# The mixer's output projection of a transformer layer: from 64 products over the whole depth to seven half-size products for each pair of token tiles

## The chip, the cores and the metric

One core of a Trainium2 chip runs the whole kernel. The metric is device time in microseconds of one execution, as the median of several. TensorE (PE) multiplies, VectorE (DVE), ScalarE (ACT) and GpSimd (POOL) compute elementwise, and SyncE (SP), ACT and POOL issue DMA transfers.

## The reference, cut to what matters

One layer: 512 prompt tokens and 8 sample tokens of width 1024, float32.

```
pool_out  = causal pooling of u, a linear map per group        # 512 columns
mlstm_out = sigmoid(og) * norm(mlstm heads) * mlstm_norm_g     # 512 columns
mix = concat([pool_out, mlstm_out]) @ w_out                    # the changed part
x = layer_norm(ALPHA * x + mix, ln1_g, ln1_b)
qc = x @ ca_wq      # cross attention follows, then a mixture of experts
```

## The kernel before

Tokens lie in five tiles: prompt tiles 0, 1, 2 and 4 of 128 rows, and tile 3 (`SAMPLES`) of 8. `mixT` holds the mixed values transposed, eight blocks of 128 channels: blocks 0 to 3 are the pooled half, written by ACT (L1516), blocks 4 to 7 the heads, written by VectorE (`take_heads`, L1979). Weights come in column blocks of 1024 x 512 (2 MB) into a ring `wring` of three slots: SP issues them in order (`block_load`, L1206), each when the block three earlier has been used. `w_out` is the blocks wo0 and wo1; the slot of block `u` is next filled with wq0.

The projection of a tile is two banks (one for each 512 columns of the output), each eight products of 128x128 by 128x512. A float32 product stands in the trace as two records. Tile 0 is written out by hand (`wo_steps`, L787): its first halves run before and after the last pooling product (`pool_product(3, 1)`, L746) and the turning of the states (`turn_states`, L757, record L761). Tiles 1, 2 and 4 use `rows_project` (L765, record L773). Between them stand the transposes of finished tiles (`transpose_x`, L541, record L548), two small ones for the samples (L812, L819), and the samples' own projection (`rows_samples`, L777, record L782). Then comes the query projection, itself seven half-size products for two halves of the tokens (`product`, L587, record L611); its product 6 needs sums of tokens (`sum_tokens`, L1790) and of weights (`sum_weights`, L1771) that VectorE makes.

VectorE takes each bank with `residual` (L2054): ALPHA times x plus the bank (L2062) and statistics of 512 columns (L1740), twice a tile, and then `norm` (L1742): aggregate (L1750), center and scale by gain (L1752), wait for GpSimd's inverse deviation (`norm_rstd`, L2550), scale and add (L1761). Between the tiles stand the samples' head output (L2082 to L2096), the samples' mixed values (L2101) and three sums of wq0. `bank_d` hands three PSUM banks (ps3 to ps5) round: PE waits until VectorE has freed the bank of three uses ago. MBANK, ps6 and ps7, is idle here.

GpSimd's program is in order: for each sample it loads a state (`load_state`, L2596: 256 KB and 512 KB), waits for VectorE's `carried` (L1984) and updates the state (`update_state`, L2603: three operations and a store). Between these stand `window_sums` (L2615), which VectorE's `pool_diff(0)` needs, and `head_rstd(3)` (L2587), which the last heads need. After sample 6 it loads the gain and bias vectors of the first norm (L2670, L2671), stores the states and loads state 7.

The order around the change comes from these in-order programs and their semaphores alone. Tile 0's start on PE is, cut:

```python
wo_steps(wo_banks[0], "wo0", (4, 5, 6, 7))
pool_product(3, 1)
turn_states()
wo_steps(wo_banks[1], "wo1", (4, 5, 6, 7))
pe.wait_ge(act_free, at["pool"])
```

## Time and profile before

| | us |
|---|---|
| three runs, median (lowest to highest) | 663.36 (663.21 to 664.26) |
| the profiled execution | 662.14 |
| its span, first to last instruction | 660.4 |
| PE busy, DVE busy, POOL busy in it | 630.5, 345.6, 204.6 |

The profiled execution's own time is 1.7 us above its span, and 1.2 us below the median. Times in rows count from the start of the span. A chain of waits follows the last instruction back to whatever released each step.

### The profile page before, as it was taken

The page shows a single profiled execution, that of the slowest core. Times are in us where ns is not written, and L with a number is a line of the kernel's source. Part 1 is how long each engine was busy: PE and PEld are TensorE (multiplying, and loading weights), DVE is VectorE, ACT ScalarE, POOL GpSimd, SP SyncE. Part 2 cuts the span into 40 slices and gives each one's busy share as a digit, 9 for nine tenths or more (in the row PEclk, how much of TensorE's full clock was granted, in tenths as well). Part 3 has the DMA queues.
Part 4 walks back from the last instruction along what each step waited for, and adds up shares of the span by engine and source line. Part 5 has one row for each costly group of instructions (what it writes and reads, how often), then busy time and mean ns, then how long its engine had stood idle before and what let it go on. Part 6 is the DMA issues. An engine that isn't in the chain of part 4 may idle for free.

```text
span 660.4 us, 8621 instructions
## 1 busy us (share of the span) xinstructions
PE 630.5 (95%) x3216; PEld 387.4 (59%) x3216; DVE 345.6 (52%) x803; ACT 152.5 (23%) x334; POOL 204.6 (31%) x240
## 2 busy tenths in 40 slices
PE   6999999999999999999999999989999999999992
PEld 3445588887888864446888774444564444333331
DVE  0283356326556960857643865355873334244465
ACT  1113221001544120002002640222324111121144
POOL 5241010100577735412002984102244432111221
PEclk9999999999999999999999999999999999999997
DMA  8994478613335357104705977544449999999797
GB/s 301 393 327 168 144 168 223 233 54 127 101 88 200 113 191 129 47 0 149 297 0 189 346 276 276 223 164 188 200 152 359 414 411 416 383 362 415 270 192 157
DMA packets 45667, 146.07 MB, mean 221 GB/s; under 512 B 5594, under 2 KB 5786, under 8 KB 41519
## 3 DMA queue, kind: packets, MB, share of 16 engines
q1 hardware_dynamic: 31847, 108.29, 44.0%
q0 software_dynamic: 11600, 32.24, 18.4%
q10 hardware_dynamic: 2176, 4.96, 2.0%
q8 instruction: 27, 0.44, 0.3%
q14 instruction: 17, 0.14, 0.1%
HBM read 130.27 MB, written 20.33 MB: 228 GB/s over the span
## 4 chain that ended last, share of the span: by engine, by line
PE 78%; DMA 9%; DVE 6%; issue 2%; POOL 2%; ACT 1%; ACTq 0%; DVEq 0%; POOLq 0%
PE ps L611 15%; PE ps L773 14%; PE ps L520 9%; PE ps L1115 7%; PE ps L484 6%; PE ps L1135 4%; PE ps L609 4%; DMA P<-x_d,smp 3%; PE ps L792 2%; DMA xn<-y_d 2%; PE ps L876 2%; PE ps L860 1%; PE ps L667 1%; PE ps L548 1%; DMA P<-in_cache_mem_v 1%
## 5 line engine op out<-in xcount | busy, mean ns | idle before, releaser
L773 PE MATMUL ps<-wring,P 128*128 128x512 f32 x224 | 99.4, 596 | 0.0
L773 PEld LDWEIGHTS ps<-wring,P 128*128 128x128 f32 x224 | 41.5, 190 | 49.4 <-issue 49.3
L1115 PE MATMUL ps<-wring,P 128*32 128x512 f32 (+1 forms) x288 | 63.6, 593 | 0.9 <-DVE P L2386 0.9
L1810 DVE SCALAR_TENSOR_TENSOR P<-ps,P 128x264 f32<-128x264 f32 (+1 forms) x70 | 28.8, 427 | 60.9 <-PE ps L611 44.3
L520 PE MATMUL ps<-wring,P 128*128 128x512 f32 x128 | 58.1, 612 | 1.0 <-DVE P L1765 0.8
L484 PE MATMUL ps<-xT,wring 128*128 128x312 f32 (+1 forms) x256 | 57.5, 383 | 0.0
L2556 POOL TENSOR_SCALAR rstd<-agg 128x1 f32<-128x1 f32 (+1 forms) x15 | 15.7, 1049 | 117.9 <-DVE agg L1750 117.9
L484 PEld LDWEIGHTS ps<-xT,wring 128*128 128x128 f32 x256 | 46.4, 190 | 9.3
L2386 DVE COPY P<-ps 128x512 f32<-128x512 f32 x11 | 7.6, 692 | 74.3 <-PE ps L1096 66.8
L520 PEld LDWEIGHTS ps<-wring,P 128*128 128x128 f32 x128 | 24.7, 196 | 31.2 <-issue 31.0
L1115 PEld LDWEIGHTS ps<-wring,P 128*32 128x32 f32 (+1 forms) x288 | 21.6, 128 | 35.0 <-issue 34.9
L2699 POOL TENSOR_TENSOR P<-P,xT 128x2048 f32<-128x2048 f32 x8 | 36.1, 4523 | 8.9 <-DMA xT<-sq_d 5.6
L2062 DVE SCALAR_TENSOR_TENSOR xn<-xn,ps 128x512 f32<-128x512 f32 x16 | 10.9, 682 | 45.0 <-PE ps L773 25.4
L1135 PE MATMUL ps<-P 128*32 128x512 f32 (+1 forms) x144 | 32.6, 594 | 0.6 <-issue 0.6
L1400 ACT ACTIVATE xT<-ps 128x512 f32<-128x512 f32 (+1 forms) x30 | 13.9, 518 | 71.6 <-PE ps L548 71.5
L611 PE MATMUL ps<-xT,wring 128*128 128x264 f32 (+1 forms) x128 | 29.6, 387 | 0.0
L611 PE MATMUL ps<-P 128*128 128x264 f32 x128 | 29.5, 385 | 0.0
L611 PE MATMUL ps<-P,wring 128*128 128x256 f32 (+1 forms) x128 | 29.2, 382 | 0.0
L1115 PE MATMUL ps<-xT,P 128*32 128x512 f32 (+1 forms) x96 | 28.2, 593 | 0.0
L611 PEld LDWEIGHTS ps<-P 128*128 128x128 f32 x128 | 24.3, 190 | 4.2
L611 PEld LDWEIGHTS ps<-xT,wring 128*128 128x128 f32 x128 | 23.8, 190 | 4.8 <-issue 1.1
L611 PEld LDWEIGHTS ps<-P,wring 128*128 128x128 f32 x128 | 24.2, 190 | 3.8
(447 smaller groups left out, 1092.3 us busy)
## 6 DMA issues: line engine op xcount, KB each, us to landing
wring<-in_w_in SPq DMA_DIRECT2D x5, 2048.0 KB, 9.7
wring<-in_w_gate SPq DMA_DIRECT2D x10, 1024.0 KB
wring<-in_w_up SPq DMA_DIRECT2D x10, 1024.0 KB
P<-in_w_down SPq DMA_DIRECT2D x10, 1024.0 KB, 12.0
P<-in_cache_mem_k SPq DMA_DIRECT2D x8, 1024.0 KB, 6.6
P<-in_cache_mem_v SPq DMA_DIRECT2D x8, 1024.0 KB, 5.1
y_d<-P POOLq DMA_DIRECT2D x1, 4160.0 KB, 31.9
wring<-in_ca_wv SPq DMA_DIRECT2D x2, 2048.0 KB, 20.9
```

Source lines behind the costliest of these rows:

```text
L484: last = mm(out, lhs(k), rhs(k), start=(k == 0), stop=(k == n - 1))
L520: last = mm(bk[:, :], memT[:, k, m * 128:m * 128 + 128], w[:, k, :], start=(k == 0), stop=(k == KC - 1))
L609: last = mm(bank[:, 0:n], x[:, k, 128 * i:128 * i + 128], w[:, k, :], start=(k == 0), stop=(k == 3))
L611: last = mm(bank[:, 0:n], w[:, k, 128 * i:128 * i + 128], x[:, k, :], start=(k == 0), stop=(k == 3))
L773: last = mm(bk[:, :], src[:, k, START[t]:START[t] + TR], w[:, k, :], start=(k == 0), stop=(k == KC - 1))
L792: last = mm(bank[:, :], mixT[:, k, 0:TR], w[:, k, :], start=(k == 4), stop=(k == 1))
L1115: last = mm(GU[p % 2][lo:lo + m, :].rearrange("p (g f) -> p g f", g=2), xgT[:, p % 3, k, lo:lo + m], gu[s][:, :, k, :], start=(k == 0), st ...
L1135: last = mm(YB[q][lo:lo + m, :], hT[:, p % 2, f, lo:lo + m], dn[s][:, f, q * 512:q * 512 + 512], start=(f == 0), stop=(f == 1))
L1400: A(xT[:, 4 * q:4 * q + 4, START[t]:START[t] + n], bk[:, 0:4 * n].rearrange("p (k c) -> p k c", k=4), ACT.Copy).then_inc(act_free, 1)
L1810: V.scalar_tensor_tensor(dst, src, scale, part, ALU.mult, ALU.add).then_inc(part_added, 1)
L2556: link(G.tensor_scalar(x, agg[0:n, 1:2], LN_EPS, None, ALU.add))
L2699: G.tensor_tensor(x, x, qb[:, b % 4:b % 4 + 1].broadcast_to([128, 2, D]), ALU.mult).then_inc(kq_done, 1)
```

## The change

The four prompt tiles become two pairs, (0, 1) and (2, 4). For a pair, the two tiles and the two halves of the depth make a 2x2 block matrix, and so do the halves of depth and of columns of `w_out`. Seven block products (four 128x128 by 128x512 products each) take the place of eight: `first`, `second` and `fourth` use the mixed values as they are, `fifth`, `sixth`, `third` and `seventh` use sums of them, which VectorE makes (`sum_mixed`, four operations a pair). The weight sums are made by DMA: SP loads a quarter of `w_out` (1 MB) into each of four places, when the keys, values and the block u there have been used, and GpSimd issues transfers that add further quarters to them: two to `wo_sums[6]`, one each to 7 and 5, and the finished sum 6 to 4. `first` and `fifth` go to MBANK and ACT copies them out. VectorE puts the seven results together with eleven operations of 512 columns for a pair, in place of four. PE starts with both `second` and both `first` products, then waits for sums 5 and 7. The load of wq0 now waits for both `fifth`. The norm vectors are issued by ACT after the states, and state 7 is loaded before the last adding transfer. `TOKENS`, the semaphores' names and the counts of `gb_in` follow suit.

```diff
+        block_at = lambda lo: view(lo, 2048, "p (k c) -> p k c", k=4)
+        wo_sums = {6: block_at(2144), 7: block_at(4224), 4: block_at(8384), 5: wring[:, 2, 0:4, :]}
+        mixed = lambda t, hf: mixT[:, 4 * hf:4 * hf + 4, START[t]:START[t] + TR]
+        spare = [view(512 * i, 512) for i in range(4)], [sgT[:, i, 0:512] for i in range(4)]
...
+        first_part, fifth_part = [view(lo, 512) for lo in (10448, 10960)], [view(lo, 512) for lo in (13540, 14052)]
+        sum_part, all_part = view(11472, 512), view(12484, 512)
+        PAIRS = ((0, 1), (2, 4))
...
+        chain_made, sums_made = sem("chain_made"), sem("sums_made")
+        T2_HALF, T2_MADE, T4_MADE, T3_P_MADE = 16, 32, 48, 32
...
-            def wo_steps(bank, name, ks):
-                w = wring[:, BI[name] % WR]
-                for k in ks:
-                    if k == 7:
-                        pe.wait_ge(dve_free, at["heads", 3])
-                    last = mm(bank[:, :], mixT[:, k, 0:TR], w[:, k, :], start=(k == 4), stop=(k == 1))
-                return last
-
-            pe.wait_ge(dve_free, at["heads", 2])
-            for name in WO:
-                use_block(name)
-            wo_banks = [bank_d() for name in WO]
-            wo_steps(wo_banks[0], "wo0", (4, 5, 6, 7))
+            wo0, wo1 = [wring[:, BI[name] % WR] for name in WO]
+            def mixed_product(bank, x, w, done):
+                for k in range(4):
+                    last = mm(bank[:, :], x[:, k, :], w[:, k, :], start=(k == 0), stop=(k == 3))
+                last.then_inc(done, 1)
+            def first(i):
+                mixed_product(MBANK[i], mixed(PAIRS[i][0], 0), wo0[:, 0:4], act_full)
...
+            def second(i):
+                mixed_product(bank_d(), mixed(PAIRS[i][0], 1), wo0[:, 4:8], dve_full)
...
+            def fifth(i):
+                pe.wait_ge(xsum_done, MIXED[i] + 1)
+                pe.wait_ge(act_free, at["first", i])
+                mixed_product(MBANK[i], mixed_sums[i][5], wo_sums[5], act_full)
...
+            def sixth(i):
+                pe.wait_ge(xsum_done, MIXED[i] + 2)
+                mixed_product(bank_d(), mixed_sums[i][6], wo_sums[6], dve_full)
+            def third(i):
+                pe.wait_ge(xsum_done, MIXED[i] + 3)
+                mixed_product(bank_d(), mixed_sums[i][3], wo1[:, 4:8], dve_full)
+            def seventh(i):
+                pe.wait_ge(xsum_done, MIXED[i] + 4)
+                mixed_product(bank_d(), mixed_sums[i][7], wo_sums[7], dve_full)
+            def fourth(i):
+                mixed_product(bank_d(), mixed(PAIRS[i][1], 1), wo_sums[4], dve_full)
+            pe.wait_ge(dve_free, at["heads", 3])
+            use_block("wo0")
+            second(0)
+            second(1)
             pool_product(3, 1)
             at["pool"] = na[0]
             turn_states()
-            wo_steps(wo_banks[1], "wo1", (4, 5, 6, 7))
             pe.wait_ge(act_free, at["pool"])
-            for name, bank in zip(WO, wo_banks):
-                wo_steps(bank, name, (2, 3, 0, 1)).then_inc(dve_full, 1)
-            rows_project(1, WO, mixT)
-            transpose_x(0, x1_ready)
+            first(0)
+            first(1)
+            pe.wait_ge(sums_made, T3_P_MADE)
+            fifth(0)
+            fifth(1)
+            used[BI["u"]] = (act_full, na[0])
+            pe.wait_ge(chain_made, T2_MADE)
+            use_block("wo1")
+            sixth(0)
             pe.wait_ge(cq_done, NS)
             bk = bank_d()
             for h in range(H):
                 last = nc.tensor.transpose(bk[0:NS, h * 128:h * 128 + 128], cq[:, h, :], ident)
             last.then_inc(dve_full, 1)
-            rows_project(2, WO, mixT)
+            third(0)
+            seventh(0)
+            pe.wait_ge(chain_made, T4_MADE)
+            fourth(0)
+            sixth(1)
+            transpose_x(0, x1_ready)
+            third(1)
+            seventh(1)
             transpose_x(1, x1_ready)
             pe.wait_ge(samples_dve, HEADS_READY)
             bk = bank_d()
@@ -819,7 +870,7 @@
                 last = nc.tensor.transpose(bk[:, h * NS:h * NS + NS], vsn[:, h * 128:h * 128 + 128], ident[0:NS, 0:NS])
             last.then_inc(dve_full, 1)
             samples_mixed = nd[0]
-            rows_project(4, WO, mixT)
+            fourth(1)
             transpose_x(2, x1_ready)
             pe.wait_ge(dve_free, samples_mixed)
             rows_samples(WO, mixT)
...
-            for i in range(3, BI["wc0"] + 1):
+            for i in range(3, BI["wq0"]):
+                block_load(i)
+            low, high = [[w[:, 0:4], w[:, 4:8]] for w in (BLOCKS[BI["wo0"]][1], BLOCKS[BI["wo1"]][1])]
+            sp.wait_ge(dve_full, at["keys", 3])
+            sp.dma_start(wo_sums[6], high[1]).then_inc(piece_in[0], 16)
+            sp.dma_start(wo_sums[7], high[0]).then_inc(piece_in[1], 16)
+            sp.wait_ge(dve_full, at["state", 3])
+            sp.dma_start(wo_sums[4], low[1]).then_inc(piece_in[2], 16)
+            sp.wait_ge(act_full, at["u", 1])
+            sp.dma_start(wo_sums[5], low[0]).then_inc(piece_in[2], 16)
+            for i in range(BI["wq0"], BI["wc0"] + 1):
                 block_load(i)
...
             take_states()
+            act.dma_start(gb[:, 0, :], a["ln1_g"][0].partition_broadcast(128)).then_inc(emb_in, 16)
+            act.dma_start(gb[:, 1, :], a["ln1_b"][0].partition_broadcast(128)).then_inc(emb_in, 16)
...
+            def copy_part(dst, bank):
+                nf[0] += 1
+                act.wait_ge(act_full, nf[0])
+                A(dst, bank[:, :], ACT.Copy).then_inc(act_free, 1)
+
+            for part in (first_part, fifth_part):
+                for i in range(2):
+                    copy_part(part[i], MBANK[i])
...
-            dve.wait_ge(gb_in, 32)
-            residual(0, x1_ready)
...
+            def sum_mixed(i):
+                (t, u), s, done = PAIRS[i], mixed_sums[i], MIXED[i]
+                V.tensor_tensor(s[5], mixed(u, 0), mixed(u, 1), ALU.subtract).then_inc(xsum_done, 1)
+                dve.wait_ge(xsum_done, done + 1)
+                V.tensor_tensor(s[6], s[5], mixed(t, 0), ALU.subtract).then_inc(xsum_done, 1)
+                dve.wait_ge(xsum_done, done + 2)
+                V.tensor_tensor(s[3], s[6], mixed(t, 1), ALU.add).then_inc(xsum_done, 1)
+                V.tensor_tensor(s[7], mixed(t, 0), mixed(u, 0), ALU.subtract).then_inc(xsum_done, 1)
+            def take_second(i):
+                x, bk = quarter_of(PAIRS[i][0], 0), full()
+                V.scalar_tensor_tensor(x, x, ALPHA, bk[:, :], ALU.mult, ALU.add).then_inc(dve_free, 1)
+                dve.wait_ge(dve_free, nf[0])
+
+            def take_first(i):
+                x = quarter_of(PAIRS[i][0], 0)
+                dve.wait_ge(act_free, at["first", i])
+                link(V.tensor_tensor(x, x, first_part[i], ALU.add))
+
+            def take_fifth(i):
+                dve.wait_ge(act_free, at["fifth", i])
+                for t in PAIRS[i]:
+                    x = quarter_of(t, 1)
...
+                link(last)
+
+            def take_sixth(i):
+                bk, x = full(), quarter_of(PAIRS[i][0], 1)
+                V.tensor_tensor(sum_part, bk[:, :], first_part[i], ALU.add).then_inc(dve_free, 1)
+                dve.wait_ge(dve_free, nf[0])
+                link(V.tensor_tensor(x, x, sum_part, ALU.subtract))
+            def take_third(i):
+                bk, x = full(), quarter_of(PAIRS[i][0], 1)
+                V.tensor_tensor(x, x, bk[:, :], ALU.add).then_inc(dve_free, 1)
...
+            def take_seventh(i):
+                bk, u = full(), PAIRS[i][1]
+                V.tensor_tensor(all_part, bk[:, :], sum_part, ALU.add).then_inc(dve_free, 1)
+                x = quarter_of(u, 0)
+                V.scalar_tensor_tensor(x, x, ALPHA, all_part, ALU.mult, ALU.add)
+                x = quarter_of(u, 1)
+                link(V.tensor_tensor(x, x, all_part, ALU.subtract))
+                statistics(u, 1)
+            def take_fourth(i):
+                bk, x = full(), quarter_of(PAIRS[i][1], 0)
+                V.tensor_tensor(x, x, bk[:, :], ALU.add).then_inc(dve_free, 1)
...
+            take_second(0)
+            take_second(1)
+            dve.wait_ge(act_free, at["pool"])
+            sum_mixed(0)
+            sum_mixed(1)
+            take_first(0)
+            statistics(0, 0)
+            take_first(1)
+            take_fifth(0)
+            take_fifth(1)
             carried(7)
-            residual(1, x1_ready)
+            take_sixth(0)
...
+            take_third(0)
+            dve.wait_ge(emb_in, 64)
+            norm(0, x1_ready, first_known=True)
...
-            residual(2, x1_ready)
+            take_seventh(0)
+            take_fourth(0)
+            norm(1, x1_ready, first_known=True, last=0)
+            statistics(2, 0)
+            take_sixth(1)
+            take_third(1)
+            norm(2, x1_ready, first_known=True)
+            take_seventh(1)
...
-            residual(4, x1_ready, between=[lambda n=n: sum_weights("wq0", n) for n in (1, 2, 3)])
+            for n in (1, 2, 3):
+                sum_weights("wq0", n)
+            take_fourth(1)
+            norm(4, x1_ready, first_known=True, last=0)
             residual_samples("mixed rows", x1_ready)
...
             update_state(4)
+            pool.wait_ge(piece_in[0], 32)
+            pool.dma_start(wo_sums[6], low[0], accum_op=ALU.add).then_inc(chain_made, 16)
+            pool.wait_ge(piece_in[1], 32)
+            pool.dma_start(wo_sums[7], high[1], accum_op=ALU.add).then_inc(sums_made, 16)
             window_sums()
             update_state(5)
             head_rstd(3, TR, NQT)
+            pool.wait_ge(chain_made, T2_HALF)
+            pool.dma_start(wo_sums[6], high[0], accum_op=ALU.add).then_inc(chain_made, 16)
             load_state(6)
+            pool.wait_ge(piece_in[2], 48)
+            pool.dma_start(wo_sums[5], high[0], accum_op=ALU.add).then_inc(sums_made, 16)
             update_state(6)
+            load_state(7)
+            pool.wait_ge(chain_made, T2_MADE)
+            pool.dma_start(wo_sums[4], wo_sums[6], accum_op=ALU.add).then_inc(chain_made, 16)
...
-            pool.wait_ge(act_full, at["states"])
-            norm_vectors("ln1_g", "ln1_b")
             states_out()
-            load_state(7)
...
-            norm_rstd(0)
             update_state(7)
-            norm_rstd(1)
             head_rstd(4, NS, H)
-            for t in (2, 4, SAMPLES):
+            for t in (0, 1, 2, 4, SAMPLES):
```

## Rows read from the trace of the kernel before

**Rows 1.** The page: busy time of the engines, and the clock in 40 slices
```profile
PE 630.5 (95%) x3216; PEld 387.4 (59%) x3216; DVE 345.6 (52%) x803; ACT 152.5 (23%) x334; POOL 204.6 (31%) x240
PEclk9999999999999999999999999999999999999997
```
**Rows 2.** Chain of waits, 195 to 340 us: start, length, what
```profile
246.72 10.30 PE ps L792 x24
257.03 13.94 PE ps L773 x32
```
**Rows 3.** Order of time on TensorE, 190 to 330 us: start, length, what, idle before
```profile
238.51 0.66 PE L699 MATMUL ps<-con,P 128*128 128x128 f32 x4 [1.11 <-DVE P L1976]
...
245.25 1.04 PE L750 MATMUL ps<-P,poolw 128*128 128x312 f32 x4
...
321.45 7.31 PE L611 MATMUL ps<-P 128*128 128x264 f32 x32
```
**Rows 4.** VectorE's groups, 262 to 322 us: count | busy us, mean ns | idle before
```profile
L1740 DVE BATCH_NORM_STATS2 st<-xn 128x6 f32<-128x512 f32 x8 | 5.6, 695 | 0.3
L1752 DVE SCALAR_TENSOR_TENSOR xn<-xn,agg,gb 128x1024 f32<-128x1024 f32 x4 | 5.5, 1369 | 0.1
L2062 DVE SCALAR_TENSOR_TENSOR xn<-xn,ps 128x512 f32<-128x512 f32 x8 | 5.4, 680 | 22.5 <-DMA gb<-in_ln_b 16.4 <-PE ps L773 6.1
L1761 DVE SCALAR_TENSOR_TENSOR xn<-xn,rstd,gb 128x1024 f32<-128x1024 f32 x4 | 5.1, 1284 | 3.7 <-POOL rstd L2557 3.7
```
**Rows 5.** Order of time on VectorE, 205 to 330 us
```profile
229.73 1.47 DVE L2009 SCALAR_TENSOR_TENSOR P<-P 128x496 f32<-128x496 f32 x1
...
236.38 0.68 DVE L2009 SCALAR_TENSOR_TENSOR P<-P 128x496 f32<-128x496 f32 x1
...
245.72 0.29 DVE L1988 CUSTOM_DVE_ANT_0 P<-P 128x128 f32<-128x128 f32 x1 [1.69 <-DMA P<-qk_d]
...
277.20 0.67 DVE L2082 TENSOR_TENSOR P<-ps,sg 8x512 f32<-8x512 f32 x1
...
280.22 0.37 DVE L2090 BATCH_NORM_AGGREGATE hagg<-hst 8x2 f32<-8x6 f32 x4
282.05 1.10 DVE L2096 TENSOR_SCALAR smp<-smp,hagg,den 8x128 f32<-8x128 f32 x4 [1.47 <-POOL den L2588]
...
291.07 0.62 DVE L2101 SCALAR_TENSOR_TENSOR P<-ps,colv,P 128x8 f32<-128x8 f32 x4
...
307.24 1.21 DVE L2072 SCALAR_TENSOR_TENSOR xn<-xn,P 8x1024 f32<-8x1024 f32 x1 [0.93 <-ACT P L1524]
...
314.07 1.22 DVE L1796 TENSOR_TENSOR P<-xT 128x1024 f32<-128x1024 f32 x1
...
320.08 0.19 DVE L1799 TENSOR_TENSOR P<-xT,P 128x32 f32<-128x32 f32 x1
```
**Rows 6.** Order of time on GpSimd, 195 to 330 us
```profile
227.19 1.03 POOL L2617 TENSOR_TENSOR P<-P 128x512 f32<-128x512 f32 x1
...
232.62 0.78 POOL L2613 DMA_DIRECT2D out<-P  x1 [0.29 <-POOL P L2611]
235.94 0.22 POOL L2587 TENSOR_SCALAR den<-hagg 128x4 f32<-128x4 f32 x1 [2.54 <-DVE hagg L1968]
...
237.26 0.82 POOL L2600 DMA_DIRECT2D P<-in_state_mlstm_C  x1
```
**Rows 7.** DMA issues: queue, count, KB each, median us from issue to landing
```profile
wring<-in_ca_wq SPq DMA_DIRECT2D x2, 2048.0 KB, 9.0
xn<-y_d POOLq DMA_DIRECT2D x6, 512.0 KB, 8.2
```
**Rows 8.** Stretches: length, busy us of PE, PEld, DVE, ACT, POOL, clock, DMA share, GB/s
```profile
242.00:244.00 2.00, 2.00 (x6) 0.80 (x6) 1.86 (x7) 0.51 (x2) 0.00 (x0) 1.00 1.00 365
244.00:246.00 2.00, 2.00 (x8) 1.14 (x7) 0.31 (x4) 0.03 (x1) 0.00 (x0) 1.00 0.99 386
...
630.00:642.00 12.00, 12.00 (x65) 4.70 (x66) 7.67 (x15) 4.70 (x9) 3.21 (x4) 1.00 1.06 202
```

More of the change, by code:

```diff
@@ L313, in layer_kernel @@
         mem_in = [sem(f"mem_in{m}") for m in range(2)]
-        wk_in = [sem(f"wk_in{q}") for q in range(3)]
+        piece_in = [sem(f"piece_in{q}") for q in range(3)]
         HALF_MEMORY, CONSTANTS = 16, 32
         ident_ready, con_in, x_in, gb_in, small_in, cache_in = [sem(s) for s in ("ident_ready", "con_in", "x_in", "gb_in", "small_in", "cache_in")]
+        chain_made, sums_made = sem("chain_made"), sem("sums_made")
+        T2_HALF, T2_MADE, T4_MADE, T3_P_MADE = 16, 32, 48, 32
         wgr_in, st_in, emb_in = sem("wgr_in"), sem("st_in"), sem("emb_in")
@@ L410, in layer_kernel @@
         SUMMED = {name: 4 * i for i, name in enumerate(("q", "k", "v", "wq0", "wq1"))}
-        TOKENS = {name: 4 if name[0] == "w" else 0 for name in SUMMED}
+        MIXED = (4, 8)
+        TOKENS = {name: 12 if name[0] == "w" else 0 for name in SUMMED}
         part_banks = [ps[6], ps[7], ps[3], ps[4], ps[5]]
@@ L516, in memory_block @@
                         if k < 6:
-                            pe.wait_ge(wk_in[k // 2], 16)
+                            pe.wait_ge(piece_in[k // 2], 16)
                         else:
@@ L1740, in statistics, with norm @@
                 return V.bn_stats(st_of(t)[:, 6 * q:6 * q + 6], xn[0:rows_of(t), t, q * 512:q * 512 + 512])
-            def norm(t, signal, finish=True, first_known=False, meanwhile=None):
+            def norm(t, signal, finish=True, first_known=False, meanwhile=None, last=1):
                 n = rows_of(t)
@@ L1747, in norm @@
                     statistics(t, 0)
-                link(statistics(t, 1))
+                link(statistics(t, last))
                 pows[0] += 1
@@ new lines, in take_second @@
+            def take_second(i):
[10 more added lines that the diff above has]
+                    x = quarter_of(t, 1)
+                    last = V.scalar_tensor_tensor(x, x, ALPHA, fifth_part[i], ALU.mult, ALU.add)
+                link(last)
@@ L2250, in list_rows @@
                 V.tensor_copy(dst[0:rows, :, n], r[:, 89:91]).then_inc(dst_ready, 1)
-            dve.wait_ge(gb_in, 64)
+            dve.wait_ge(gb_in, 32)
             def choose_now(n):
@@ L2661, in _ @@
                 masks(h + 2)
+            low, high = [[w[:, 0:4], w[:, 4:8]] for w in (BLOCKS[BI["wo0"]][1], BLOCKS[BI["wo1"]][1])]
             update_state(4)
+            pool.wait_ge(piece_in[0], 32)
+            pool.dma_start(wo_sums[6], low[0], accum_op=ALU.add).then_inc(chain_made, 16)
+            pool.wait_ge(piece_in[1], 32)
+            pool.dma_start(wo_sums[7], high[1], accum_op=ALU.add).then_inc(sums_made, 16)
             window_sums()
```

15 lines of the change are left out of this document (12 added, 3 removed).

## The prediction

> **What bounds the kernel now.** I read the page first: TensorE is busy 95% of the span, at the full granted clock in all slices but the last [rows 1]. The chain of waits confirms it around the change: it runs on TensorE from 246.72 to 270.97 us with nothing between the products, 32 records (16 products) in 13.94 us [rows 2]. The order of time on TensorE then gives the dates: the last wait before the stretch is 1.11 us at 238.51, for VectorE's last heads; the fourth pooling product stands at 245.25; and product 6 of the query projection, the first that needs sums from VectorE, starts at 321.45 without a wait [rows 3]. VectorE's order of time shows how near it is to that date: its last token sum starts at 320.08 and takes 0.19 [rows 5]. So VectorE has 1.2 us in hand there and no more, although it is idle for 22.5 us before its reading of the banks [rows 4]: idle early, on a stalled norm vector, and nearly full late. Its late load is what decides this change, along with the transfers.
>
> I make the sum for the start of product 6, because everything after it hangs on TensorE as before and should move with it.
>
> **TensorE.** A product costs 13.94/16 = 0.87 or 10.30/12 = 0.86 us [rows 2]; four cost 3.45. Eight fewer save 6.9. Now second(0) starts at 241.8 (3.45 before the pooling product of 245.25 [rows 3]), both seconds end at 248.7, the pooling product takes 1.04 and the turning of the states 0.43 (from 246.29 to 246.72, where products go on [rows 2, 3]). The old order had four products between the states and the wait for ACT's copy of the pooled half. Now only the states cover it; the copy I put at 0.6, an estimate below VectorE's 0.68 for 512 columns [rows 4], so 0.2 us of wait appear and first(0) starts at 250.3. Both firsts end at 257.2, fifths at 264.1, sixth(0) at 267.6 if nothing is late. By TensorE alone product 6 would start at 321.45 - 6.9 + 0.2 = 314.75.
>
> **VectorE.** From the end of sixth(0) its program is dense. Its work up to the last token sum:
> - fourteen operations of 512 columns at 0.70 with their waits for themselves (0.680 each [rows 4]): 9.8. Before, the whole projection had eight such operations; now it has twenty-two, eight of them earlier
> - seven statistics of 0.695 [rows 4]: 4.9
> - four norms: aggregate 0.21 with its gap, 1.30, a wait of 3.7/4 = 0.9 for GpSimd, 1.28 [rows 4]: 14.7
> - the samples' head output, 277.20 to 280.59, 3.4, and its scaling 1.0 (four records in 1.10): 4.4; mixed values of samples 0.62 [rows 5]
> - three sums of wq0 at 1.22 (the same shape as the 1.22 of 314.07 [rows 5]): 3.7
> - the sample rows and two parts of the query product, 307.24 to 314.07 [rows 5]: 6.8
> - the sums from 314.07 to 320.27 [rows 5]: 6.2
>
> That is 51.1. From 267.6 it ends at 318.7, and at 318.9 with the stops at the banks that I get by laying both programs side by side. TensorE would be there at 314.75. So VectorE becomes the bound: 4.1 of the 6.7 us are lost to it, as waits of TensorE for the samples' mixed values before the samples' projection, for the bank of fourth(1) and the norm of tile 4, and before product 6. With transfers in time the gain is 321.45 - 318.9 = 2.5.
>
> The early operations (two seconds, eight sums, two firsts, one statistics, four of the fifths) are hidden in the idle time of 16.4 us [rows 4]. They start late, though, behind carried(6); see below.
>
> **The transfers.** No transfer adds in this stretch before. The nearest rows are the adding ones at the end (512 KB each): between 630 and 642 us the 16 engines are full (share 1.06) and move 202 GB/s, where plain loads move 365 and 386 [rows 8]. 1 MB (1.049) then costs 5.2 us to add and 2.75 to load. Bounds: 2.75 below, as if adding were free; above, the 8.2 us to landing of half a MB [rows 7], so 16. I take 5.2, the rate of full engines, since these will be full too.
>
> GpSimd's order now: update 4 ends at 227.1 (the next record stands at 227.19 [rows 6]), then the first part of sum 6 and sum 7 are issued, some 0.8 to 1.0 each as its other issues [rows 6]. window_sums and update 5 come 2.0 later, update 5's store is issued by 235.4 instead of 233.4 and head_rstd(3), which waits for VectorE until 235.94 [rows 6], is still not delayed: this part costs nothing by 0.5 us. Then the second half of sum 6, state 6, sum 5 and only then update 6. On the engines, from 229.1 (2 us after the issue): four adding MBs before the fifths may start (6, 7, 6, 5) 20.8; two loads (4 and 5) 5.5; update 5's store 0.7; state 6, 0.79 MB, 2.1. That is 29.1, so 258.2. ACT issues the norm vectors (1 MB) at about 251 on its own queue; if they share, half of them, 1.4, come ahead; landing takes 0.7: sum 5 is there at 260.3. The fifths were due at 257.2. **TensorE waits 3.1 us there**, and since VectorE's dense part starts behind sixth(0), all of it counts.
>
> That queues share is what state 6 shows before: issued at 237.26 [rows 6], beside wq0's 2 MB at 9.0 us to landing [rows 7], it released VectorE only at 245.72 [rows 5], when both together, 2.9 MB at 375 GB/s, had had their 7.7 us. The Trainium skill ("DMA: Bandwidth & Descriptors", Queues, rings and completion order) says that an engine goes round its queues packet by packet. By strict order of issue instead, sum 5 would be 1.4 us earlier and the time 662.6.
>
> State 6 itself now lands near 253.7, carried(6) ends at 254.6, the seconds are read by 256.0 and the first sum is made by 256.7, in time for 260.3. Eight sums end at 261.6, the fifths are read by 269.5 and carried(7) is done by 270.4, just before sixth(0) ends at 270.7. State 7 waits for update 6's store, which stands behind sum 5 (about 261), is issued by 263 and takes 2 + 2.1: landing at 267, for a need at 269.5. The load of wq0 starts at 267 instead of 237 and is needed near 300; 9.0 us to landing hide it. Sum 4 (from SBUF, bounded as above) is issued near 264 and due at 278. The norm vectors are due at 276. SP's waits hold back only its own pieces and wq0.
>
> Beside update 6, VectorE's operations can be slower: L2009 took 1.47 with GpSimd at work and 0.68 without [rows 5]. For the eight sums I put up to 3 us on this, and it eats the slack before carried(7) but not more; for update 7 beside the samples' work I add 0.3. The Trainium skill ("SBUF — State Buffer", Who interferes with whom) says that a VectorE instruction with two SBUF inputs contends with a GpSimd one that reads SBUF; the trace agrees (1.47 against 0.68), and by the rule without slack the time would be 2 to 3 us higher.
>
> **Sum.** The count of 51.1 gives 318.7 + 3.1 + 0.3 = 322.1 against 321.45, +0.65; with the stops at the banks it is 322.3, +0.85. I take the count: 662.14 + 0.65 = 662.8 for the profiled execution. It stood 1.2 below the median of the runs, so 664.0.
>
> **Rivals.**
> - *The transfers are in time.* Adding at 4.4 us for a MB or less brings sum 5 to 257. VectorE's dense part alone bounds: -2.5, 660.8. For it: the share of 1.06 [rows 8] counts packets of other transfers too, and the 202 GB/s may hold waits. Against: 202 GB/s was steady over 12 us.
> - *The adding transfers are slower (the other side).* Their rows are of 2 KB, half of what the measured ones carry. At 5.8 us for a MB sum 5 lands 2.4 later, at 262.7, and TensorE waits 5.5 before fifth(0): 666.4. It decides from 261.0 on: 0.7 us beyond my date are enough to be measurably slower. For it: head, store and state transfers stand in the same queue, and every delay of one is handed to the next; against: with smaller pieces the plain loads are as fast.
> - *TensorE alone bounds*, since the sums or the transposes leave VectorE more room than I count: 321.45 to 314.75, 656.7. Against it stands the 1.2 us of slack [rows 3, 5] which fourteen operations where eight stood (and the norm of tile 0 behind them) must use up.
>
> **Numbers.** About 0.2% (1.3 us) is what a measurement of this kernel can tell from no change, so 662.0 to 664.7. The forecast (wait of 2 to 4.2 us, 662.9 to 665.1) 0.38, of which 0.32 lies within 0.2% and 0.06 above; slower transfers 0.33; transfers in time 0.22; TensorE alone 0.07. That gives faster 0.29, same 0.32, slower 0.39. The range of 8 in 10 takes in the transfers in time down to 660.4 and the slower ones up to 667.6 (a wait of 6.7), and leaves out TensorE alone and the rest of the slower ones.
>
> **What would show it.** In the profile after: the idle time before fifth(0) on TensorE, released by the adding transfer into the slot of u, 3 us (0 and over 5 are the rivals); carried(6) near 254; VectorE without idle time but for GpSimd's inverse deviations from sixth(0) on; waits of TensorE for VectorE before the samples' projection, the query's first product and product 6. If product 6 starts before 317 or no wait is seen in front of it, the count of VectorE's work is wrong; if heads 3 starts later than 238.5, so is the claim that GpSimd's two issues are free.

## The result and the profile after

The changed kernel took 673.29 us (median of 5 runs, 671.81 to 681.25) where the kernel before took 663.36 (660.39 to 667.97): a ratio of 1.0166, 95% interval 1.0126 to 1.0207. That is slower than the forecast, than its range and than the price of the rival on the slow side. A run over 1.5% above the fastest of its kernel is left out of the ratios and of the medians given here; of the changed kernels only experiment 2 has one (678.55 us). The profiled execution was the longest of the five. At 330 us it is 1.1 us behind the profile of the unchanged repeat below, which took 673.3; the rest of its excess lies behind 430 us, outside the change (a wait of 2.48 us for a sample's value cache that the repeat has not, and a granted clock of 0.91 from 500 to 540 us, where the repeat has 1.00).

The page of the changed kernel, the lines that answer to [rows 1]:

```profile
PE 636.0 (94%) x3200; PEld 389.5 (57%) x3200; DVE 364.2 (54%) x825; ACT 155.1 (23%) x338; POOL 210.5 (31%) x243
PEclk9999999999999988998999999989989999999996
```

TensorE has 16 records fewer (8 products of two records), and yet is busy 5.5 us longer. A good part of that belongs to this long execution: in the repeat it is busy 629.8 us, 0.7 less than before, where eight products fewer are worth 6.9. The clock line says why one must not read "busy" as "work": apart from the last slice, which was low before too, five slices are below 0.90. Those of 238 to 272 and 306 to 323 us lie at the change, the two behind 430 us outside it. The order of time on TensorE shows which records paid (start, length, what, idle before):

```profile
241.51 1.12 PE L710 MATMUL ps<-con,P 128*128 128x128 f32 x4 [3.38 <-DVE P L2048]
242.42 3.07 PE L761 MATMUL ps<-P,poolw 128*128 128x312 f32 x8
...
254.80 7.13 PE L803 MATMUL ps<-wring,P 128*128 128x512 f32 x16
266.34 9.95 PE L803 MATMUL ps<-wring,P 128*128 128x512 f32 x16 [4.41 <-DMA wring<-in_w_out]
...
309.64 5.27 PE L793 MATMUL ps<-wring,P 128*8 128x256 f32 x64 [2.09 <-DVE P L2246]
...
330.76 7.41 PE L622 MATMUL ps<-P 128*128 128x264 f32 x32
```

Product 6 of the query projection starts at 330.76, against 321.45 in [rows 3]: 9.3 us, nearly the whole 9.9 of the times (0.7 of it stood already at 205 us, ahead of the change). In the repeat it is 8.2 of 9.2. Three waits are seen: 3.38 for VectorE's heads (1.11 before), 4.41 for weight sum 5, 2.09 for the samples' mixed values. Behind the second the same 16 records that took 7.13 at 254.80 take 9.95. The stretches of the changed kernel (length, busy us of PE, PEld, DVE, ACT, POOL, clock, DMA share, GB/s):

```profile
240.00:244.00 4.00, 2.49 (x8) 2.12 (x9) 2.17 (x7) 0.23 (x1) 1.41 (x2) 0.66 1.08 288
252.00:256.00 4.00, 3.85 (x15) 2.19 (x14) 0.00 (x0) 1.39 (x3) 1.30 (x1) 1.00 0.61 215
256.00:260.00 4.00, 4.00 (x10) 1.71 (x9) 3.72 (x12) 0.60 (x1) 2.72 (x3) 1.00 1.01 254
260.00:264.00 4.00, 1.94 (x5) 0.57 (x3) 3.93 (x5) 0.60 (x1) 1.74 (x2) 1.00 1.10 200
264.00:268.00 4.00, 1.66 (x2) 0.84 (x3) 3.30 (x6) 0.00 (x0) 0.72 (x1) 0.65 0.48 123
268.00:272.00 4.00, 4.00 (x6) 1.69 (x5) 0.00 (x0) 0.00 (x0) 4.00 (x8) 0.50 0.87 251
```

Behind both long waits TensorE runs for a while at its lower level, 0.50 of full speed, 1.2 of 2.4 GHz: the mean of 240 to 244 is 0.66, and behind the wait for sum 5 it is 0.50 through all of 268 to 272. At that level there are 6 records in the 4 us, where 272 to 276 at full clock has 10.

The chain of waits tells which of the three waits led to the end:

```profile
231.11 7.03 PE ps L495 x32
238.16 16.14 DMA wring<-in_w_out
254.30 0.37 issue
254.67 11.63 DMA wring<-in_w_out
266.34 13.39 PE ps L803 x24
279.76 0.70 DVE P L2178
```

It does not pass through the heads at all. It leaves TensorE at 238.16, when the block u is done and SP may load quarter 5 into its place, goes with that load for 16.14 us, with the adding transfer into it for 11.63, through fifths and sixth(0), and then onto VectorE, as forecast. GpSimd's order of time shows what it did meanwhile:

```profile
229.13 1.29 POOL L2815 DMA_DIRECT2D P<-in_w_out  x1 [0.48 <-DMA P<-in_w_out]
229.91 1.58 POOL L2765 TENSOR_TENSOR P<-P 128x512 f32<-128x512 f32 x1
230.91 1.57 POOL L2757 TENSOR_TENSOR P<-P,wcb 128x512 f32<-128x512 f32 x1
231.91 1.56 POOL L2758 TENSOR_TENSOR P<-P,vsT 128x512 f32<-128x512 f32 x1
...
246.33 0.79 POOL L2748 DMA_DIRECT2D P<-in_state_mlstm_C  x1 [4.92 <-DMA out<-P]
...
254.67 1.30 POOL L2823 DMA_DIRECT2D wring<-in_w_out  x1 [6.98 <-DMA wring<-in_w_out]
```

It waits 4.92 us for the store of update 5, which stands behind adding transfers, 6.98 for load 5 and, at 267.28, 5.24 for the store of update 6. Beside the three operations from 229.91 to 233.47, one operation of VectorE, which took 1.47 in [rows 5], takes 4.67:

```profile
229.35 4.67 DVE L2081 SCALAR_TENSOR_TENSOR P<-P 128x496 f32<-128x496 f32 x1
```

The transfers issued between 220 and 285 us (queue, count, KB each, median us to landing):

```profile
P<-in_w_out SPq DMA_DIRECT2D x3, 1024.0 KB, 8.1
P<-in_w_out POOLq DMA_DIRECT2D x3, 1024.0 KB, 14.0
...
wring<-in_w_out SPq DMA_DIRECT2D x1, 1024.0 KB, 16.1
...
wring<-in_w_out POOLq DMA_DIRECT2D x1, 1024.0 KB, 11.6
```

A plain load of 1 MB takes 16.1 us here, where wq0's 2 MB took 9.0 in [rows 7]. Sum 5's own transfer is the last row, issued at 254.67. What the queues moved from 256 to 260 us (packets, MB, share) shows that it hardly ran in that time; q10 carries the norm vectors that ACT issued at 254.70 and 255.08, q0 is GpSimd's:

```profile
q10 hardware_dynamic: 265, 0.99, 96.1%
q0 software_dynamic: 15, 0.03, 4.9%
```

### The profile page after: what moved, and what is told of

The parts are those of the page before. It is cut to its first block, busy times and chain, and to the rows that moved or that the text cites. A ratio compares the mean times of both kernels' runs of the same rounds, so it can differ in the third digit from the quotient of the medians.

```text
span 679.5 us, 8634 instructions
## 1 busy us (share of the span) xinstructions
PE 636.0 (94%) x3200; PEld 389.5 (57%) x3200; DVE 364.2 (54%) x825; ACT 155.1 (23%) x338; POOL 210.5 (31%) x243
## 4 chain that ended last, share of the span: by engine, by line
PE 78%; DMA 9%; DVE 7%; issue 2%; ACT 1%; POOL 1%; DVEq 0%; ACTq 0%; POOLq 0%
PE ps L622 15%; PE ps L1166 11%; PE ps L531 9%; PE ps L495 8%; PE ps L784 7%; PE ps L1186 5%; DMA wring<-in_w_out 4%; PE ps L620 4%; DMA xn<-y_d 2%; PE ps L803 2%; PE ps L927 2%; DMA P<-in_cache_mem_v 2%; PE ps L911 1%; PE ps L1147 1%; PE ps L693 1%
## 5 line engine op out<-in xcount | busy, mean ns | idle before, releaser
L1166 PE MATMUL ps<-wring,P 128*32 128x512 f32 (+1 forms) x288 | 65.4, 600 | 0.9 <-DVE P L2534 0.9
L531 PE MATMUL ps<-wring,P 128*128 128x512 f32 x128 | 58.7, 617 | 1.0 <-DVE P L1837 0.8
L784 PE MATMUL ps<-wring,P 128*128 128x512 f32 x128 | 58.7, 609 | 0.0
L531 PEld LDWEIGHTS ps<-wring,P 128*128 128x128 f32 x128 | 24.9, 198 | 31.6 <-issue 31.3
L784 PEld LDWEIGHTS ps<-wring,P 128*128 128x128 f32 x128 | 24.0, 194 | 28.3 <-issue 28.2
L803 PE MATMUL ps<-wring,P 128*128 128x512 f32 x64 | 31.3, 644 | 4.6 <-DMA wring<-in_w_out 4.4
L2870 POOL DMA_INDIRECT P<-x_d,smp x11 | 11.3, 1031 | 47.4 <-PE ps L1147 28.1
```

What stands on the lines that cost most here:

```text
L531: last = mm(bk[:, :], memT[:, k, m * 128:m * 128 + 128], w[:, k, :], start=(k == 0), stop=(k == KC - 1))
L784: last = mm(bk[:, :], src[:, k, START[t]:START[t] + TR], w[:, k, :], start=(k == 0), stop=(k == KC - 1))
L803: last = mm(bank[:, :], x[:, k, :], w[:, k, :], start=(k == 0), stop=(k == 3))
L1166: last = mm(GU[p % 2][lo:lo + m, :].rearrange("p (g f) -> p g f", g=2), xgT[:, p % 3, k, lo:lo + m], gu[s][:, :, k, :], start=(k == 0), st ...
```

## The experiments

Each was run beside the kernel before on the same chip, so ratios are against that. "Heads" is the start of the first record of L710 (TensorE's turning of the last heads). Where a kernel leaves something out, its expectation says so.

**1. The changed kernel once more**, no edit.

> The changed kernel once more, to have a typical profile of it. Both theories: 672 us, with the same three waits of TensorE (about 3.4 us before the last heads, 4.4 before fifth(0), 2 before the samples' projection). If each of these waits is followed by a stretch at half the clock again, the lowered clock belongs to the waits; if the heads come back to 238.5 us, the 3 us lost there were chance.

Measured: 673.20 us, ratio 1.0119 (1.0050 to 1.0187). The heads start at 240.56, not at 238.5. The heads' wait is 3.13 us, that for sum 5 is 4.67 with 9.71 us for the 16 records behind it, and product 6 starts at 329.62. The picture repeats. One thing differs: behind the same wait of 2.09 us the samples' projection takes 3.64 us at full clock, not 5.27, and yet product 6 is as late behind it (21.13 us from start to start, 21.12 in the first profile), because TensorE then waits for VectorE instead. This third loss of clock costs nothing.

**2. No wait for the weight sums**, all transfers still made.

```diff
-                mixed_product(MBANK[i], mixed_sums[i][5], wo_sums[5], act_full)
+                mixed_product(MBANK[i], mixed_sums[i][5], wo0[:, 0:4], act_full)
...
-            pe.wait_ge(sums_made, T3_P_MADE)
...
-            pe.wait_ge(chain_made, T2_MADE)
...
-            pe.wait_ge(chain_made, T4_MADE)
```

The sixths, sevenths and fourths take plain quarters in the same way. So that no quarter is overwritten too early, the edit also adds waits for the sums elsewhere: SP waits for sums 5 and 7 ahead of wq0 and for sum 4 ahead of wq1, and VectorE for sum 4 ahead of its sums of wq0, which it starts at 302.02 without a wait.

> All loads and adding transfers run as in the change, but TensorE multiplies by plain quarters of w_out and waits for no sum, so the projection's values are not the reference's. My theory (the wait for the adding transfers, 4.4 us, and the half clock behind it, 3 us more, are the larger part of the loss): no wait before fifth(0), no lowered clock there, 7 us less than the changed kernel, 665. Rival (the traffic and GpSimd's issues slow the kernel by themselves, and the wait only stands where VectorE would have been late anyway): 670 or more.

Measured: 667.31 us, ratio 1.0048 (1.0010 to 1.0085). TensorE:

```profile
240.21 1.12 PE L710 MATMUL ps<-con,P 128*128 128x128 f32 x4 [3.12 <-DVE P L2048]
241.12 3.67 PE L761 MATMUL ps<-P,poolw 128*128 128x312 f32 x8
...
254.81 17.43 PE L803 MATMUL ps<-wring,P 128*128 128x512 f32 x40
...
323.29 2.06 PE L622 MATMUL ps<-P 128*128 128x264 f32 x8 [0.17 <-DVE P L1871]
```

The wait before the fifths and its lowered clock are gone, and product 6 moves from 329.6 to 323.3: 6.3 us. The heads stay late, with another VectorE operation held, one of 16 columns this time:

```profile
228.69 4.15 DVE L2082 TENSOR_TENSOR P<-P 128x16 f32<-128x16 f32 x1
```

**3. No weight sums at all**: as 2, and the four loads and five adding transfers are left out.

```diff
-            pool.dma_start(wo_sums[6], low[0], accum_op=ALU.add).then_inc(chain_made, 16)
...
-            pool.dma_start(wo_sums[7], high[1], accum_op=ALU.add).then_inc(sums_made, 16)
```

> As plain_quarters, and the four loads and five adding transfers are left out too, so the values are not the reference's. My theory: the heads are back at 238.5 us after a wait of 1.1, state 6 lands by 246, and only VectorE's dense program of 51 us behind sixth(0) bounds: 661 (2.5 us below the kernel before). Rival (VectorE's added operations alone make the change lose): 664 or more, with the heads at 238.5.

Measured: 661.31 us, ratio 0.9962 (0.9934 to 0.9990).

```profile
238.94 0.66 PE L710 MATMUL ps<-con,P 128*128 128x128 f32 x4 [1.30 <-DVE P L2038]
...
298.08 5.33 PE L793 MATMUL ps<-wring,P 128*8 128x256 f32 x64 [2.09 <-DVE P L2236]
...
320.05 7.31 PE L622 MATMUL ps<-P 128*128 128x264 f32 x32
```

This is the case that the prediction called "the transfers are in time", priced at 660.8. So the products and VectorE's part were priced well, and all of the loss hangs on how the sums are made: 673.2 to 667.3 by the waits for them, 667.3 to 661.3 by their traffic and issues. The date of product 6 is less of a proof: VectorE's last token sum ends at 319.14, and product 6 starts 0.9 later, since TensorE lost 1.7 us to the clock on the samples' projection (5.33 for 3.64) and waited 0.66 for a block of wq.

**4. The price of a wait by itself**: the kernel before, with TensorE waiting for the norm vectors ahead of tile 1's products.

```diff
+            pe.wait_ge(gb_in, 32)
```

> The kernel before, in which TensorE waits for the norm vectors before tile 1; they landed at 263.0, when it would start at 256.9, and VectorE has room behind it. If a wait of this size also costs clock: 6 us for the wait and some 3 us for a stretch at half the clock behind it, 672. Rival (the half clock in the changed kernel comes from something else than the wait): 6 us alone, 669.5, at the full clock.

Measured: 671.99 us, ratio 1.0133 (1.0071 to 1.0195).

```profile
262.00 17.01 PE L773 MATMUL ps<-wring,P 128*128 128x512 f32 x32 [4.21 <-DMA gb<-in_ln_b]
```

The same records in the order of time of the kernel before:

```profile
256.86 14.10 PE L773 MATMUL ps<-wring,P 128*128 128x512 f32 x32
```

The wait is 4.21 us, and the 32 records behind it take 2.9 us more, by the clock. A wait of 4.2 us costs 7.1; the times differ by 8.0.

**5. The first two adding issues behind the heads' deviations**: experiment 2 with this move on GpSimd.

```diff
             update_state(4)
-            pool.wait_ge(piece_in[0], 32)
-            pool.dma_start(wo_sums[6], low[0], accum_op=ALU.add).then_inc(chain_made, 16)
-            pool.wait_ge(piece_in[1], 32)
-            pool.dma_start(wo_sums[7], high[1], accum_op=ALU.add).then_inc(sums_made, 16)
             window_sums()
             update_state(5)
             head_rstd(3, TR, NQT)
+            pool.wait_ge(piece_in[0], 32)
+            pool.dma_start(wo_sums[6], low[0], accum_op=ALU.add).then_inc(chain_made, 16)
+            pool.wait_ge(piece_in[1], 32)
+            pool.dma_start(wo_sums[7], high[1], accum_op=ALU.add).then_inc(sums_made, 16)
```

> This is plain_quarters (sums of the changed order, TensorE taking plain quarters and waiting for no sum, all adding transfers made) with GpSimd's first two adding issues moved behind head_rstd(3); nothing else differs. My theory: what delays heads 3 by some 1.5 us and more is that these two issues push update 5 against VectorE's work on heads 3, where one VectorE operation of 16 columns was held for 4.1 us; the traffic itself does not slow VectorE. Then heads 3 start near 238.9 as in no_sums, the pooling products run at full clock, and the time is about 664, some 4 below plain_quarters. Rival (the adding traffic slows VectorE or the chip, wherever it is issued): heads 3 stay near 240.5, the clock falls in the same slices and the time stays near 667.5.

Measured: 673.45 us, ratio 1.0137 (1.0094 to 1.0180). The step that it tested came out as I said: VectorE's operations are not held,

```profile
230.33 0.90 DVE L2080 TENSOR_TENSOR P<-P,con 128x16 f32<-128x16 f32 x1
231.26 1.47 DVE L2081 SCALAR_TENSOR_TENSOR P<-P 128x496 f32<-128x496 f32 x1
```

and the heads (at 240.51, the rival's date, but this execution was 1.5 us behind experiment 2's already) follow their predecessors (the first record of L710 one head earlier) by 12.8 us, where it is 14.0 in experiment 2 and 12.2 in experiment 3; behind their wait of 1.91 us the pooling products keep the full clock (1.98 us). My sum for the time was wrong by 9 us, since I left out what the moved issues stand in front of: 

```profile
250.62 1.28 POOL L2821 DMA_DIRECT2D P<-in_w_out  x1 [9.12 <-DMA P<-in_w_out]
251.36 1.31 POOL L2749 DMA_DIRECT2D P<-in_state_mlstm_C  x1
```

State 6 is issued 5 us later than in the changed kernel and lands in 13.3 us, not 9.0. VectorE waits 19.41 us for it to 265.43, makes the sums of mixed values behind it, and TensorE waits 9.66 for those, with half the clock afterwards. A state for which VectorE waits 1.69 us in the kernel before [rows 5], at no cost there, is the bound here.

**6. Less work for VectorE behind sixth(0)**: experiment 3 without six operations of 512 columns.

```diff
-                link(V.tensor_tensor(x, x, sum_part, ALU.subtract))
...
-                V.scalar_tensor_tensor(x, x, ALPHA, all_part, ALU.mult, ALU.add)
-                x = quarter_of(u, 1)
-                link(V.tensor_tensor(x, x, all_part, ALU.subtract))
```

> This is no_sums without six of VectorE's 512-column operations behind sixth(0): the second operation of the sixths' reading and two of the sevenths', in each pair; 6 x 0.70 = 4.2 us less work for VectorE, TensorE's products and all transfers as in no_sums. My theory (VectorE's dense program from the end of sixth(0) sets when product 6 of the query projection can start): product 6 starts 2.5 to 4.2 us earlier than the 320.05 of no_sums and the time is about 657.5. Rival (VectorE's work is not what bounds there, the waits seen are of another chain): product 6 stays within 1 us of 320.05 and the time near 661.

Measured: 657.53 us, ratio 0.9905 (0.9870 to 0.9941), 3.8 below experiment 3 for 4.2 us of work.

```profile
295.79 3.64 PE L793 MATMUL ps<-wring,P 128*8 128x256 f32 x64
...
315.36 4.85 PE L622 MATMUL ps<-P 128*128 128x264 f32 x21
```

No wait stands before the samples' projection any more, and VectorE's last token sum ends at 315.10, not 319.14: 4.0 us for 4.2 us of work. VectorE bounds up to that projection, which starts 2.3 us earlier. Product 6 comes 4.7 us earlier; the other 2.4 are the lowered clock and the wait for wq of experiment 3, both gone here.

**7. The sums by the engines**: GpSimd makes sums 7, 6 and 4, VectorE sum 5; the results are the changed kernel's.

```diff
+            G.tensor_tensor(wo_sums[7], wo1[:, 0:4], wo1[:, 4:8], ALU.add)
...
+            G.tensor_tensor(wo_sums[6], wo_sums[7], wo0[:, 0:4], ALU.add)
+            G.tensor_tensor(wo_sums[4], wo_sums[6], wo0[:, 4:8], ALU.add)
...
+            V.tensor_tensor(wo_sums[5], wo0[:, 0:4], wo1[:, 0:4], ALU.add)
```

> The changed kernel without the transfers for the sums: GpSimd makes sum 7 behind load_state(6), sums 6 and 4 behind load_state(7), in its idle time, and VectorE makes sum 5 in its own before the firsts. The products, their order and the results are those of the changed kernel. My theory (the transfers are what costs; the products by sums are worth a small gain): no wait before fifth(0), no lowered clock, product 6 near 320 and the time about 661.5, as no_sums. Rival (GpSimd's 2048-column sums hold VectorE, or come too late for the fifths and sixths): waits of 1 us and more before the fifths or sixths, product 6 after 321.5 and 664 or more.

Measured: 674.25 us, ratio 1.0146 (1.0114 to 1.0178): the rival. One operation of GpSimd,

```profile
238.34 4.50 POOL L2818 TENSOR_TENSOR P<-wring 128x2048 f32<-128x2048 f32 x1
```

and VectorE's beside it and beside the two later ones:

```profile
237.01 6.70 DVE L2042 TENSOR_SCALAR P<-P,hagg,den 128x128 f32<-128x128 f32 x4
...
265.96 4.51 DVE L2161 TENSOR_TENSOR xn<-xn,P 128x512 f32<-128x512 f32 x1 [1.02 <-ACT P L1589]
270.50 4.89 DVE L2167 SCALAR_TENSOR_TENSOR xn<-xn,P 128x512 f32<-128x512 f32 x1
```

The same operations take 1.12 and 0.69 us in experiment 3. Here the first ends at 243.71, 0.9 behind the end of GpSimd's (242.84), and the second at 270.47, 0.6 behind that of GpSimd's next sum (265.38 and 4.52 long): VectorE is not slowed but stopped. (Its first group is 5.6 us longer than in experiment 3, 1.1 more than GpSimd's operation lasts; no run shows why.) TensorE waits 6.71 us for the heads and runs at half clock behind it. The Trainium skill ("SBUF — State Buffer", SBUF: two separate sides) calls the ports that VectorE and GpSimd share an exclusive lock, kept for a whole instruction; these ends agree.

**8. The same with VectorE's waits filled**: work is put where it waited for GpSimd's inverse deviations.

```diff
-            norm(0, x1_ready, first_known=True)
+            norm(0, x1_ready, first_known=True, meanwhile=scale_heads)
...
-            norm(1, x1_ready, first_known=True, last=0)
-            statistics(2, 0)
+            norm(1, x1_ready, first_known=True, last=0, meanwhile=lambda: statistics(2, 0))
...
+            norm(2, x1_ready, first_known=True, meanwhile=lambda: read_seventh(1))
```

> engine_sums with work of VectorE put into its waits for GpSimd's inverse deviation: the samples' head scaling into the norm of tile 0, the samples' statistics into that of tile 1, the reading of seventh(1) into that of tile 2. My theory (from sixth(0) to product 6 VectorE bounds, and 0.9 us of each norm is a wait that can hold work): product 6 some 2 to 2.5 us earlier than in engine_sums, about 659.3. Rival (TensorE or the heads of the samples bound there, or the moved work delays what TensorE waits for): as engine_sums, 661.5.

Measured: 670.78 us, ratio 1.0093 (1.0067 to 1.0120). The level is wrong as in 7, the difference right: heads to product 6 is 83.6 us against 85.7, 2.1 less, and the times 3.5 less.

**9. All four sums by VectorE in its own idle time.**

```diff
             take_heads(3)
+            V.tensor_tensor(wo_sums[7], wo1[:, 0:4], wo1[:, 4:8], ALU.add)
...
             take_second(1)
+            V.tensor_tensor(wo_sums[5], wo0[:, 0:4], wo1[:, 0:4], ALU.add)
...
+            V.tensor_tensor(wo_sums[6], wo_sums[7], wo0[:, 0:4], ALU.add)
             take_fifth(0)
+            V.tensor_tensor(wo_sums[4], wo_sums[6], wo0[:, 4:8], ALU.add)
             take_fifth(1)
```

> engine_sums with all four sums made by VectorE, in its own idle times (sum 7 behind the last heads, sum 5 behind the second second, sum 6 ahead of the fifths' reading, sum 4 inside it): 4 operations of 2048 columns at 2.2 us as L2200 of engine_sums, which was 2.58 with the wait for itself. Products, their order and the results are those of the changed kernel; no transfer and no GpSimd work for the sums. In no_sums these idle times are 1.2, 2.8, 2.8 and 2.1 us. My theory (a VectorE operation is held only by GpSimd's work beside it, and the idle times hold the sums): heads 3 near 238.9 (12.2 us behind heads 2), no wait of TensorE before the fifths and sixths, sixth(0) ends near 268.3, product 6 near 320.3, the time 661.5 (660 to 663), 0.3% below the kernel before. Rival (update 6 of GpSimd beside sum 5, or the later pool window, delays the fifths or the last pooling product by over 1 us, or the clock falls): 664 and more.

Measured: 663.60 us, ratio 1.0011 (0.9983 to 1.0039).

```profile
240.14 0.66 PE L709 MATMUL ps<-con,P 128*128 128x128 f32 x4 [2.08 <-DVE P L2040]
240.64 3.36 PE L760 MATMUL ps<-P,poolw 128*128 128x312 f32 x8
...
322.06 7.41 PE L621 MATMUL ps<-P 128*128 128x264 f32 x32
```

The sums fit (2.28 to 2.29 us each, no wait of TensorE for them), but the heads' wait was 2.08 in this execution and the clock fell behind it, 3.36 for 1.98 and 1.23 for 1.04. The heads follow their predecessors by 12.9 us here, though no sum stands ahead of them. The time lies 0.6 above my range of 660 to 663 and below the rival's 664, and the ratio can't be told from no change.

**10. Both together**: 9 with the filling of 8.

> vector_sums with VectorE's waits for GpSimd's inverse deviation filled as in engine_sums_filled, where heads 3 to product 6 became 2.1 us shorter. My theory: product 6 near 318.2 and the time 659.4, 0.6% below the kernel before and 2.1 below vector_sums. Rival (with VectorE ahead, the load of the next weight block or TensorE itself bounds, of which no_sums showed a wait of 0.66 for the load): within 0.7 of vector_sums.

Measured: 660.16 us (12 runs, 656.48 to 662.88), ratio 0.9952 (0.9926 to 0.9979), and some 13 us below the changed kernel by the medians of two chips (11 to 14 by the ratios).

```profile
239.93 0.65 PE L709 MATMUL ps<-con,P 128*128 128x128 f32 x4 [1.14 <-DVE P L2040]
240.42 1.98 PE L760 MATMUL ps<-P,poolw 128*128 128x312 f32 x8
...
318.01 7.41 PE L621 MATMUL ps<-P 128*128 128x264 f32 x32
```

Product 6 starts 3.4 us ahead of [rows 3], near the 318.2 of my theory. With the change's products and results, and its sums made elsewhere, it beats both kernels, the one before by 0.5%. This profiled execution (662.09) is one of the longest of the twelve; its granted clock was 0.91 from 440 to 460 us and 0.83 from 480 to 500. Against 9 it is 3.8 us shorter from heads to product 6, of which 1.6 are the clock on the pooling products, which 9 lost by its late heads; so the filling is worth 2.2 by the traces, where the medians differ by 3.4. The kernel before with such filling wasn't run. TensorE has no wait for VectorE in its stretch [rows 2, 3], so I expect nothing from it, but that isn't shown.

## Why the prediction was wrong, point by point

- **TensorE's part was right.** A product costs 0.87 (experiment 2: 40 records, 20 products, in 17.43), the copy of the pooled half gave a wait of 0.15 (254.05 and 0.60, then 254.80), and in experiment 3, with no transfer in the way, sixth(0) ends at 268.2, where I had 267.6 for nothing late.
- **VectorE's count was right.** From the end of sixth(0), 279.76, to its last token sum at 330.7 it is 51.0 us; I had 51.1. Experiment 6 shows by removal that it bounds up to the samples' projection, and 3 that the case without waits is worth 661.3 (forecast for it 660.8). In my test of the count, "no wait is seen in front of it", the place was wrong: no wait stands in front of product 6 in the changed kernel, where it starts at 330.76 and VectorE's last token sum ends at 330.71. The waits stand further ahead, before the samples' projection and, in the repeat, behind it (0.53 and 0.57).
- **The failed step is the date of sum 5**, "sum 5 is there at 260.3", by which TensorE would wait 3.1. It landed at 266.3: 6.0 later. The rate of 202 GB/s was not what failed; 200 GB/s at a share of 1.10 is what the row for 260 to 264 has. What failed is that I let the engines work without a gap on 29.1 us of transfers from 229.1 on, in which it does not matter which bytes come first. In fact sum 5's adding transfer needs load 5, which could only be issued at 238.16 and shared the engines with adding transfers until 254.30. By my sum everything ahead of that last MB was done at 253.0 (258.2 less 5.2), so this is 1.3 of the 6.0. Then the last link stood alone, and it took 12.0 us from 254.30 to 266.34, where my sum has 7.3 (5.2, 1.4 and 0.7). GpSimd issued it 0.4 later. The engines stood at a share of 0.20 between 254 and 256, some 1.3 us from the issue on. From 256 to 260 they carried the norm vectors and nearly nothing else: 4.0 us, where I had let 1.4 come ahead. From 260 on, 1.28 MB (with the store of update 6) took 6.3 us with the landing, where I had 5.9. No run shows the landing's 0.7 by itself. The terms that failed are thus the norm vectors' share (2.6 us), the start of the last link (1.7), which I had at nothing, and what stood ahead of it (1.3).
- **The second failed step is what a wait costs.** I priced the wait at its length. The 16 records behind it took 9.95 instead of 7.0, 2.9 more. With the 6.0 that is 8.9, and sixth(0) ends at 279.7 instead of 270.7, a difference of 9.0. Experiment 4 shows the same without anything of the change: 4.21 of wait, 2.9 of clock.
- **"This part costs nothing" was wrong, and hidden.** GpSimd's two issues made the heads 2 to 3 us late (241.51; I had named 238.5 as the test). I had looked at GpSimd's own slack. What moved was which VectorE operation its next ones met, and that one was held for 4.67. In the changed kernel this cost nothing more, since the chain runs by load 5 and not by the heads. In experiment 2 it is what is left, together with the traffic: heads behind heads in 14.0 us for 12.2, and 2.3 us of clock on the pooling products (3.67 for 1.98, 1.68 for 1.04). Experiments 2 and 5 tell the hold from the traffic: with the issues moved it is gone, most of the lateness too. What the traffic takes of the 6.0 us between 2 and 3 beyond that isn't settled; their two profiled executions differ by only 2.6.
- **The rival on the slow side** had the place right (the wait before fifth(0), 5.5 us by it, 4.4 and 4.7 measured, with the firsts themselves late) and the mechanism wrong: it blamed the rate. Its 666.4 lacked the clock.
- **State 6** let VectorE go on at 256.2, not 253.7; the fifths waited longer for sum 5, so that cost nothing. Experiment 5 shows what it costs when it is later still.
- The Trainium skill ("DMA: Bandwidth & Descriptors", Queues, rings and completion order) has an engine take its queues in turn, packet by packet. From 246 to 250 us the trace agrees: GpSimd's queue and SP's moved 255 packets each, and load 5 took 16.1 us, 7 longer than twice its bytes did in [rows 7]. I drew on the rule for the norm vectors only, and there it did not come out: their queue moved 265 packets from 256 to 260 and GpSimd's 15. In the repeat it is 132 to 22 from 253.5 to 258. Whether GpSimd's packets were not there yet or were passed over, no run shows.

## What to carry to other kernels

Price a chain of dependent transfers link by link, each with issue, landing and what shares the engines or comes ahead in its own interval; a total of bytes over a rate dates only the last of independent ones. Price a wait of several microseconds on a saturated TensorE at its length plus the slower records behind it, here 3 us for 4. Where one engine has idle time in front of the place that needs a result, a vector operation of 2.3 us there can beat a transfer that takes no engine's time but its issue: here by 7 to 10 us by the ratios, with 2 to 3 more from filling waits.

## What was not expected of the hardware

- **Which waits the clock fell behind.** Before the pooling products, TensorE's waits of 1.11 [rows 3], 1.14, 1.15, 1.30, 1.44 and 1.91 us left the products at their 1.98 us; behind 2.08, 3.12, 3.13, 3.38, 6.71 and 6.80 the clock fell. It fell behind the waits of 4.21, 4.41, 4.67 and 9.66 too. Behind the wait of 2.09 before the samples' projection it fell in two profiles (5.27 and 5.33 us) and didn't in five (3.64). And behind 2.76 and 2.60 before the samples' small transposes (experiments 7 and 8) it stayed at 1.00. The length of a wait alone does not decide.
- **A small operation can be the one that is held.** 16 columns took 4.15 us beside three GpSimd operations of 512 columns (experiment 2), where the same takes 0.17 alone. It ended at 232.84, with the third of them (232.80). These operations stand close behind GpSimd's own issues of adding transfers; they start 1.0 us apart and last 1.57 each, overlapping, and in that row of three VectorE got no turn.
- **One operation of 2048 columns** takes 2.3 us on VectorE and 4.5 on GpSimd, and on GpSimd it held VectorE's operations beside it for 3.8 to 5.6 us (experiment 7).
